# Moving the second layer's late modulation into the first context tile's attention, and alternating the order of the expert groups in layer 0

## The reference, cut to what matters

```python
for l in range(DEPTH):                      # DEPTH = 2
    sh_a, sc_a, gt_a, sh_f, sc_f, gt_f = split(silu(c) @ w_mod[l] + b_mod[l])     # w_mod[l]: 1024 x 6144
    ... the same for c_ctx, which modulates the context tokens
    hl = rmsnorm(xl) * (1 + sc_a) + sh_a;   xl = xl + gt_a * (mixers(hl, hc) @ w_out[l])
    hl = rmsnorm(xl) * (1 + sc_f) + sh_f;   xl = xl + gt_f * experts(hl)
    # context tokens likewise, in layer 0 only
def experts(h):                             # 16 experts, each takes its 64 best latent (32 best context) tokens
    gates, idx = top_k(softmax(h @ w_router))
    y = (silu(xs @ w_gate) * (xs @ w_up)) @ w_down * gates   # three 1024 x 1024 matrices for each expert
```

## Time and profile before

| | us |
|---|---|
| median of 3 runs (2144.3 to 2151.32) | 2147.86 |
| the profiled execution | 2151.53 |
| its span | 2149.7 |
| attention of layer 0, first scores to last | about 272 to 583 |
| gather and transposes before the experts of layer 0 | 632.7 to 645.4 |
| the 48 expert stages of layer 0 | 645.4 to 1187.5 |
| the 48 expert stages of layer 1 | 1674.9 to 2123.3 |

### The profile page before, as it was taken

The page is one execution under the profiler, slowest core; times in us unless marked ns, Lnnn a source line. Parts: engine busy times, 40 slices in busy tenths (PEclk is TensorE's granted clock), DMA queues, the critical chain, the costliest instruction groups (busy, mean ns, idle before and its releaser), DMA issues. The chain is left out here.

```text
span 2149.7 us, 27244 instructions
## 1 busy us (share of the span) xinstructions
PE 1969.2 (92%) x10872; PEld 931.5 (43%) x10872; DVE 664.1 (31%) x1746; ACT 529.6 (25%) x1222; POOL 156.6 (7%) x155
## 2 busy tenths in 40 slices
PE   5999989999979999999999899889997998888875
PEld 2436465556642332323323556455554333333322
DVE  3322345666540100101001632366665011110203
ACT  3211154665531000100100421165554110000001
POOL 1101010000010010020100101100001000000000
PEclk9999979999989999999999999999998999999998
DMA  9742020000089999999999402020017899999995
GB/s 353 291 159 81 0 79 1 1 2 1 36 332 414 423 364 418 378 390 421 364 414 421 150 20 79 17 82 1 21 40 286 352 427 426 426 427 427 427 427 217
DMA packets 90935, 515.66 MB, mean 240 GB/s; under 512 B 10594, under 2 KB 15628, under 8 KB 36540
## 3 DMA queue, kind: packets, MB, share of 16 engines
q1 hardware_dynamic: 84496, 493.29, 56.8%
q0 software_dynamic: 4416, 15.21, 2.4%
q10 hardware_dynamic: 1900, 5.43, 0.6%
HBM read 498.69 MB, written 15.20 MB: 239 GB/s over the span
## 5 line engine op out<-in xcount | busy, mean ns | idle before, releaser
L739 PE MATMUL psS<-arena 128*64 128x512 f32 (+9 forms) x4552 | 1158.5, 556 | 71.1 <-DMA arena<-in_w_up 22.0
L739 PEld LDWEIGHTS psS<-arena 128*64 128x64 f32 (+4 forms) x4552 | 456.1, 159 | 666.9 <-issue 585.9
L1961 DVE TENSOR_REDUCE mx<-psS 128x1 f32<-128x768 f32 (+2 forms) x200 | 165.5, 827 | 153.0 <-PE psS L739 151.3
L1307 ACT ACTIVATE arena<-psT 128x768 f32<-128x768 f32 (+7 forms) x261 | 150.1, 577 | 245.7 <-PE psT L742 232.0
L742 PE MATMUL psT<-ident,arena 128*128 128x128 f32 (+1 forms) x1036 | 172.7, 290 | 36.1 <-ACT arena L1307 9.1
L1307 ACT ACTIVATE arena<-psS 128x128 f32<-128x128 f32 (+5 forms) x158 | 61.8, 421 | 571.6 <-PE psS L739 525.7
L2145 DVE TENSOR_TENSOR arena<-arena,psS 128x512 f32<-128x512 f32 x32 | 20.6, 684 | 549.2 <-PE psS L739 549.2
L742 PEld LDWEIGHTS psT<-ident,arena 128*128 128x128 f32 (+1 forms) x1036 | 120.1, 145 | 135.5 <-issue 97.8
L739 PE MATMUL psT<-arena 128*32 128x512 f32 x1536 | 174.5, 595 | 0.0
L1307 ACT ACTIVATE arena<-psS,nb 128x768 f32<-128x768 f32 (+2 forms) x200 | 157.9, 792 | 1.4
L739 PE MATMUL psM<-arena 128*128 128x512 f32 x288 | 140.9, 611 | 0.0
(11 more groups left out here) (226 smaller groups left out, 1266.5 us busy)
## 6 DMA issues: line engine op xcount, KB each, us to landing
arena<-in_w_gate SPq DMA_DIRECT2D x117, 1024.0 KB, 21.3
arena<-in_w_up SPq DMA_DIRECT2D x116, 1024.0 KB, 22.5
arena<-in_w_down SPq DMA_DIRECT2D x116, 1024.0 KB, 25.9
arena<-in_w_mod SPq DMA_DIRECT2D x48, 1024.0 KB, 7.2
arena<-in_w_in SPq DMA_DIRECT2D x6, 2048.0 KB, 7.8
arena<-in_w_out SPq DMA_DIRECT2D x8, 512.0 KB, 7.8
arena<-in_w_out SPq DMA_DIRECT2D x2, 2048.0 KB, 15.4
normed_rows<-arena ACTq DMA_DIRECT2D x8, 512.0 KB, 7.3
```

The source lines that it names most:

```text
L739: return nc.tensor.matmul(o, lhsT, rhs, start=start, stop=stop)
L1307: return nc.scalar.activation(o, i, f, **kw)
L1961: link(V.reduce_max(mx[:, par:par + 1], view(S, 0, P, 0, (512, 2), (1, n)), axis=AX.XY))
```

## The change

1. The 16 late chunks no longer pass through the expert ring. They are loaded into four slots in `w_out`'s place, from the end of the projections on, and multiplied at steps 0 to 11 of the first context tile's attention. ACT copies their rows at steps 6 and 12, PE and DVE turn them at steps 16 and 24. `w_out` is loaded after them, part by part, as the slots come free.
2. The router's bias moves from steps 3 and 5 to 7 and 8, layer 0's gates from 7, 9, 11, 13 to 9, 11, 13, 15.
3. In layer 0's expert stages the order of the groups alternates. A stage that begins with the context group waits for all four loads at once. The transposes of the hidden rows and of the next tokens are moved to match, the latter in pairs; ACT and DVE follow the new order 2, 0, 1 of the hidden tiles.
4. `AHEAD_OF_GATHER` goes; in layer 1 the last two slots of the ring wait for the second gather instead.

```diff
-GATE_AT = ((7, 9, 11, 13), (9, 11))
-BIAS_AT = ((3, 5), (7,))
+GATE_AT = ((9, 11, 13, 15), (9, 11))
+BIAS_AT = ((7, 8), (7,))
-LAST_MOD_AT = {"turn": 13, "columns": 14}
+LATE_AT = {0: (0, 1), 1: (2, 3), 2: (4,), 3: (5,), 4: (6,), 5: (7,), 7: (8, 9), 8: (10, 11), 9: (12,), 10: (13,), 11: (14, 15)}
+LATE_ROW_AT = {6: 0, 12: 1}
+LATE_TURN_AT = {TURNS: 0, TURNS + 8: 1}
+LATE_BANK, LATE_TURN_BANK = (7, 5), 5
+LATE_SLOTS = 4
-TURN_AT = {(8, 1): (0,), (8, 2): (1,), (9, 0): (2,), (9, 1): (3,), (9, 2): (4,), (10, 0): (5,), (10, 1): (6,), (10, 2): (7,)}
+CLL, LLC = (2, 0, 1), (0, 1, 2)
+HIDDEN_AT = {(7, 0): 2, (7, 1): 0, (8, 2): 1}
+STAGE_ORDER = (LLC, CLL, LLC, CLL, LLC, CLL, LLC, CLL, CLL, LLC, CLL, LLC)
+TURN_AT = {(8, 1): (0, 1), (9, 1): (2, 3), (10, 2): (4, 5), (11, 1): (6, 7)}
...
+                def late_chunk(c):
+                    _, r, k = MOD_CHUNKS[MOD_FRONT * KD + c]
+                    if c >= LATE_SLOTS:
+                        sp.wait_ge(s_mused, MOD_FRONT * KD + c - LATE_SLOTS + 1)
+                    load(ar[:, late_slot(c):late_slot(c) + SLOT], A["w_mod"][L - 1, k * P:(k + 1) * P, r * 2048:(r + 1) * 2048], s_w[c % 8])
...
+                if l == 0:
+                    sp.wait_ge(z["proj"], NSTEP - TT)
+                    for c in range(2):
+                        late_chunk(c)
                 sp.wait_ge(z["proj"], NSTEP)
+                if l == 0:
+                    for c in range(2, 2 * KD):
+                        late_chunk(c)
+                for n, k in enumerate((4, 6, 0, 2)):
+                    if l == 0:
+                        sp.wait_ge(s_mused, (MOD_FRONT + 2) * KD - LATE_SLOTS + n + 1)
...
                     if l and j == NSLOT[l] - 2:
                         sp.wait_ge(z["fgev"], 4 * L)
+                        sp.wait_ge(s_g[1], 16 * L)
-                    if l == 0 and j == FIRST[l] + AHEAD_OF_GATHER:
-                        sp.wait_ge(s_g[2], 16)
...
+                    for c in LATE_AT.get(s, ()) if l == 0 else ():
+                        if c == KD:
+                            pe.wait_ge(z["me"], turns_through(PLANS[l], ("Q", 1, "B1")))
+                        late_mod(c)
+                    if l == 0 and s in LATE_TURN_AT:
+                        g = LATE_TURN_AT[s]
+                        pe.wait_ge(z["me"], turns_through(PLANS[l], ("Q", 2, "B1") if g else ("Q", 1, "C1")))
+                        mod_transpose(MOD_FRONT + g, LATE_TURN_BANK)
...
                     for x in turns:
+                        if l == 0 and x == ("Q", 1, "D"):
+                            pe.wait_ge(s_mrow, MOD_FRONT + 2)
+                        if l == 0 and x in (("T", 0, None), ("Q", 2, "D")):
+                            pe.wait_ge(s_mcol, MOD_FRONT + (1 if x[0] == "T" else 2))
                         turn(*x, values=v)
...
                         experts, n, col = range(QUAD), CAP_C, 256
-                        for e in experts if (q, st) == (NQ - 1, NSTAGE - 1) else ():
+                        for e in experts if order(l, q, st)[0] == g else ():
                             pe.wait_ge(*slot_filled(l, (q * NSTAGE + st) * QUAD + e))
...
+                    if l == 0 and s in LATE_ROW_AT:
+                        modulation_row(LATE_ROW_AT[s])
```

More of the change, by code:

```diff
@@ L596, in _ @@
                              A["w_router"][k].rearrange("(q p k) e -> p q (k e)", p=P, k=2), s_x)
+                if l == 0:
+                    sp.wait_ge(z["proj"], NSTEP - TT)
+                    for c in range(2):
+                        late_chunk(c)
                 sp.wait_ge(z["proj"], NSTEP)
[L599 to L606, removed]
+                if l == 0:
[4 more added lines that the diff above has]
+                        sp.wait_ge(s_mused, (MOD_FRONT + 2) * KD - LATE_SLOTS + n + 1)
+                    w = A["w_out"][l, k * P:(k + 2) * P, :]
+                    if k in (0, 6):
+                        for b in range(2):
+                            load(view(ar, 64 * b, 64, WOUT + k * D, (D, 2), (1, D)),
+                                 w[128 * b:128 * b + 128, :].rearrange("(a p) n -> p a n", p=64), z["wo"])
+                    else:
+                        load(ar[:, WOUT + k * D:WOUT + (k + 2) * D].rearrange("p (k n) -> p k n", k=2),
+                             w.rearrange("(k p) n -> p k n", p=P), z["wo"])
+                for j in range(NLOAD):
                     if j in OPEN[l]:
@@ L616, in _ @@
                         sp.wait_ge(z["fgev"], 4 * L)
+                        sp.wait_ge(s_g[1], 16 * L)
                     if l == 0 and j == NSLOT[l] - 1:
                         sp.wait_ge(s_xd, 16 * TT)
-                    if l == 0 and j == FIRST[l] + AHEAD_OF_GATHER:
-                        sp.wait_ge(s_g[2], 16)
                     last = j - NSLOT[l]
[L622 to L628, removed]
-                        load(ring(l, j), A["w_mod"][L - 1, k * P:(k + 1) * P, r * 2048:(r + 1) * 2048], s_w[j % NSLOT[l]])
-                        continue
-                    n = j - FIRST[l]
+                    if last >= 0:
+                        st, e = divmod(last, QUAD)
+                        sp.wait_ge(z["done"], groups_done(l, 0, st, e // 2) if l else stage_done(l, 0, st))
+                    n = j
                     if l == 0 and n == SUMS_STORED_AT * QUAD:
@@ L1164, in _ @@
                 gates(5, "fg", (0, 1, 2, 3))
-                late = range(MOD_FRONT * KD, (MOD_FRONT + 1) * KD) if l == 0 else ()
-                for n in late[:6]:
-                    late_mod(n)
                 pe.wait_ge(z["fgev"], 4 * l + 4)
                 for n in range(2):
-                    if n and l == 0:
-                        late_mod(late[6])
                     pe.wait_ge(z["dup"], 2 * l + n + 1)
                     tr(bank(4 + n, 0, P, 0, 48), ar[0:48, F["DUP"] + n * P:F["DUP"] + n * P + P], 48).then_inc(z["dupT"], 1)
-                for n in late[7:]:
-                    late_mod(n)
-                for g in (MOD_FRONT,) if l == 0 else ():
-                    mod_transpose(g, late_bank(g))
                 wc = l == 0
@@ L1210, in turn_hidden @@
                         last.then_inc(z["hp"], 1)
[L1211 to L1213 removed]
+                        free[6 + b] = (z["he"], 2 * hidden_turn(l, q, g) - 1 + b)
                 def combine(q):
@@ L1235, in combine @@
                         free[b] = (z["ce"], c * len(CJ) + n + 1)
-                    for m in last_late[4:] if l == 0 else ():
-                        late_mod(m)
                 def group(q, st, g):
@@ L1284, in _ @@
                     for st in range(NSTAGE):
-                        for g in last_order(l) if (q, st) == (NQ - 1, NSTAGE - 1) else range(NX):
-                            if st == 8 and g == 1 and wc:
-                                turn_hidden(q, 2)
+                        for g in (last_order(l) if not wc and (q, st) == (NQ - 1, NSTAGE - 1) else order(l, q, st)):
                             group(q, st, g)
-                            if st == 7 and g == 1:
+                            if wc and (st, g) in HIDDEN_AT:
+                                turn_hidden(q, HIDDEN_AT[st, g])
+                            if not wc and st == 7 and g == 1:
                                 turn_hidden(q, 0)
-                            if st == 7 and g == NX - 1:
                                 turn_hidden(q, 1)
@@ L1596, in _ @@
                 for q in range(NQ):
-                    for g in range(NX):
+                    for g in hidden_order(l):
                         act.wait_ge(z["done"], groups_done(l, q, 3, g))
@@ L2112, in _ @@
                         link(last)
-                for g in (MOD_FRONT,) if l == 0 else ():
-                    mod_columns(g, late_bank(g))
-                    dve.wait_ge(s_mcol, g + 1)
                 dve.sem_inc(z["lgev"], 1)
```

97 lines of the change are left out of this document (44 added, 53 removed).

## The result

The changed kernel takes 2164.41 us (median of 5 runs, 2161.1 to 2168.04), the kernel before 2147.86 beside it: ratio 1.007, 95% interval 1.0053 to 1.0086. That is 16.5 us slower. The forecast was 2152, with a range up to 2163, so the median lies 1.4 us beyond the range.

What follows compares the result with a forecast made beforehand. PE narrowly bounds layer 0's experts with DMA full, transfers bound layer 1's, a PE-DVE-ACT chain the first attention. 8.5 + 4.5 - 0.3 - 3.5 - 3.9 - 0.9 = +4.4 on 2151.5 gives 2155.9, as a median 2152; range 2139 to 2163.

Steps and rivals of the forecast that it cites:

- A: First tile's attention: taking in the late modulation costs +8.5 us, bounds +5 and +17.
- B: Layer 0's experts: alternation saves 7.7 us but adds waits for fourth loads; +4.5 us net, from -7.7 to +8.
- rival 2: First tile costs double, by clock at 0.50 or chunk waits: +17 there, step 12 above 317, 2161 us; chance 0.22.
- 16 - 3 - 3: First tile: 16 us of late work, less 3 for the router's bias moved, less 3 for the clock returning sooner.
- early recovery: First tile: denser work from step 0 brings the clock back before 292, 3 us off.
- the last lands at 306.0 at the earliest: First tile: with chunks 2 and 3 issued at 269.2, the last chunk lands at 306.0; 1.5 us charged for waits.
- Rival 1: Layer 0's experts: fourth loads arrive in time, alternation pays in full, -7.7 us, total 2140; chance 0.25.
- PE leads by only 0.7 us a stage: Layer 0's experts: a plain stage takes PE 10.6 us, its four loads 9.85 us.
- C: Seam at 1189, in `combine`: late chunks leave, PE idles 3.9 us and the clock may fall; -0.3 us, bounds -2.3 and +0.4.
- D: Token gathers before the experts: faster on a free queue, -3.5 us in layer 0 and -3.9 in layer 1.
- E: Layer 1: ACT's copy of 0.59 leaves a waiting chain, four transposes leave PE; -0.9 us.
- Rival 3: Gathers gain nothing, since their time is their own and not the queue's; sum +11.8 us, 2160; chance 0.08.

Runs made afterwards that it cites:

- late_only: The changed kernel with the alternation in layer 0's experts taken back; 2156.72 us, ratio 1.0043 to the kernel before.
- early_release: The changed kernel, with slots of experts 0 and 1 freed after the first latent group in context-first stages; 2167.36 us.
- late_narrow: late_only with all pieces multiplied, but over 64 columns instead of 512 in 12 of 16 late chunks; 2156.78 us.
- two_in_one: The changed kernel with narrow, 256 KB late chunks, context-first stages 1, 7, 8, 10 and silu in the order stage 3 ends; 2156.44 us.
- alt_only: The kernel before with the alternation alone; 2153.48 us, ratio 1.0028.
- guard_only: The kernel before, with layer 1's last two loads of the first ring filling waiting for both gathers; 2146.11 us, ratio 0.9991.
- late_light: late_only with only one of four pieces multiplied in 14 of 16 late chunks; 2156.82 us.
- late_small: late_only with late chunks of 256 KB instead of 1 MB, all matmuls kept; 2154.05 us.
- best1: guard_only with context-first stages 1, 9 and 11 of each quad and token turns in pairs; 2144.85 us, ratio 0.9986.
- before_half: The kernel before, with layer 0's expert loads bringing half their bytes from stage 4 of quad 0 on; 2141.97 us.
- alt_half: alt_only with layer 0's expert loads bringing half their bytes from stage 4 of quad 0 on; 2132.31 us.
- best2: guard_only with context-first stages 1, 7, 8, 10 and the changed kernel's places for hidden tiles and token turns; 2151.01 us, ratio 1.0010.

## Why the prediction came out as it did

**The sum.** The forecast was +4.4; it came to +16.5. The direction that I gave 0.34 happened. Two additions in the prediction are wrong: A's terms, 16 - 3 - 3 - 3 + 0.9 + 1.5, make 9.4 and not 8.5, and B's four quads, 1.1 + 1.1 + 0 + 2.1, make 4.3 and not 4.5. Put right, the forecast is 0.7 higher, which explains little of the miss. Term by term:

**A, late modulation in the first tile: +8.5 predicted, +13 measured** (325.4 against 312.3 to the end of attention; one by one +10.1, +13.3 and +16.0 in after, late_only and early_release). The mechanism stood: step 12 moved from 32 to 43 us after the first scores. At 316.15 it is 3 us past the announced 311 to 313 and just under rival 2's 317; in late_only and early_release it came at 316.9 and 319.2, 44.5 and 48.7 us after the first scores.

The small terms held. PE's waits for chunks were 1.9, 2.2 and 2.0 us for the 1.5 charged, its wait for the row copy 0.84 for 0.9. The other idle time up to step 12 fell from 3.7 to 1.5 us, where 3 were taken off. What was mis-sized is "16 - 3 - 3": PE's busy time up to step 12 is 28.4 us before and 39.0, 40.5 and 44.9 us in the three, so +10.5, +12.1 and +16.5 for that +10: near it in after, not in the others. The three execute the same matmuls there; what differs is the granted clock, 0.96, 0.92 and 0.82 in the mean of the stretch (0.68 before). Windows of PE from step 0's scores to step 12, before, then after, late_only and early_release:

```profile
271.68:303.94 32.26, 28.43 (x181) 0.68 0.45 126
```

```profile
273.46:316.15 42.69, 38.96 (x310) 0.96 0.94 369
```

```profile
272.39:316.93 44.54, 40.49 (x311) 0.92 0.91 355
```

```profile
270.56:319.22 48.66, 44.89 (x310) 0.82 0.87 327
```

The early recovery came, but the clock didn't stay: in 302 to 308 it was 1.00 in after, 0.74 in late_only and 0.72 in early_release. So a part of rival 2 is in the number. Why the clock falls in one execution and not in another stays open.

The stream was mis-sized too, in "the last lands at 306.0 at the earliest". In late_narrow chunk 15 was multiplied, on landing, at 311.78, although little PE work stood in its way. I had let the stream run from 269.2 on. But with four slots the fifth chunk can go out only when PE has multiplied the first, near 278, and the engines run short until then: 302 GB/s in 272 to 278 and 339 in 278 to 284 there, 115 in 278 to 282 in after, 425 and more only behind that. In after itself this bound isn't what PE waits for behind 290.

The experiments show two bounds that lie close together. With the stream shortened, 40.4 us are left to step 12; with PE's work shortened, 41.7; with both, 33.3. Each number is one execution, against 42.6 to 48.7 for the chunks in full size, and late_narrow has its 6 us at 1.2 GHz in it, so the first two are rough; 33.3 stands clear of the rest. It rules out that row copies, moved gates and moved turns make the 13 us. It doesn't show that they are free: two_in_one is 1 us above the kernel before, with the clock at 0.95 in the mean up to step 12 against 0.68, and with some late work left.

The other side of A held too: where the late work came from it had been free. From the end of attention to the first of the two top-k transposes all executions take 44.5 us, with or without the six chunks of 5.36 us; and from `combine` to layer 1 they take 17.3 to 18.4 against 17.9. So 16 chunks left places where PE waited for others, and came to one where it had no 13 us to spare.

**B, alternation: +4.5 predicted, +7.8 measured** (quads 550.1 in the mean of after, alt_only and early_release, 542.3 of before, guard_only and late_only; late_light, late_small and late_narrow, in the old order too, have 542.6 to 545.4). Its gain was as said, 7.7 against 8.4 with half loads. The Trainium skill, page "TensorEngine Tiling (Array Packing)", section Key Properties, says that a change of tiling mode drains the engine and gives no price. That a change costs something agrees with the traces: 8.4 us over 44 changes and the paired turns put it below 0.2 us each. The single waits held as well: 2.7 foretold at stage 7 of quad 0, 2.59; 2.7 at stage 5 of quads 1 and 2, 3.23 and 2.52; 2.8 at stage 7 of quad 3, 2.58. What was mis-sized is the sum of the costs. I took 12.2 us (4.5 and the 7.7 saved); the new waits alone are 13.9 in after, with 0.9 and 1.2 at stage 3 of quads 1 and 3, which I hadn't counted, and 1.7 more for the clock after the wait at 985.31. Rival 1, by which the loads would be there, is out.

There is a rule behind it that the prediction had only in part ("PE leads by only 0.7 us a stage"). From the first full point of quad 1 to that of quad 2 it is 136.0 us before (828.53 to 964.57), 137.0 in best1, 135.8 in two_in_one, 137.1 in alt_only (its waits at stage 5) and 137.5 in after. PE's savings, 3 to 8 us in the four quads and so 1 to 2 in this period, don't shorten it. early_release shows that issue isn't the limit at these points, and the window before 731.11 shows 429 GB/s. Over the whole period the DMA engines are busy for 0.98 before and 0.97 to 0.99 in the others, that is for 133 to 134 us in each. So in layer 0, too, the stream sets most of a quad's length, and PE chooses where it waits. The 1 to 4 us beside that stand for the most part in one place (share 0.80 in 890 to 910 before, 0.78 in after); what holds the stream there no run tests. Why the quads of two_in_one are 4 us longer than best1's is not settled; the waits at stage 7 of quads 0 and 3 (2.59 and 2.58), which best1 doesn't have, may be it, but no run tells them apart.

**C, the seam: -0.3 predicted.** From `combine` to layer 1's first transposes 17.28 us in after against 17.91, 17.3 to 18.4 in the others. PE idled 3.73 us at 1209.62, the clock fell to 0.53 in 1211 to 1214, as foretold (all had moved by 16 us), but for some 3 us and not 6.

**D, the gathers: -3.5 and -3.9 predicted.** Layer 0: from the top-k to the first expert matmul 12.0 to 12.4 us in after, late_only and early_release, 14.3 to 14.5 in before, guard_only and alt_only: -2.3. (Of the other four without the change, best1, before_half and alt_half have 13.8 to 14.0, best2 16.8.) The three gathers landed in 5.6 us after issue instead of 7.1, not in the announced 3.5 to 5, and PE waited 0.44 more for the second.

Layer 1, with E's copy and transposes in it: PE's wait was 4.8 to 5.3 us in every execution with the edit, near the announced 4 to 5, and 6.0 to 8.4 in the four without it. But from the first transposes of the layer to the first expert matmul it is 464.9 us in after, 466.7 in late_only and 466.8 in early_release, against 469.4 in before, 468.6 in alt_only, 468.3 in before_half and 465.4 in alt_half: -1.8 in the mean, for the -4.8 of D and E. The step that failed is that a shorter wait brings the experts' start forward by as much; executions differ by 2 us ahead of the wait, so -1.8 is rough. Rival 3 is out, and both terms were too hopeful, the second by more.

With these sizes, 13 + 7.8 - 0.3 - 2.3 - 1.8 = 16.4, near the 16.5 of the medians. With executions that differ by several us in A alone, that it meets so well is partly luck.

## What to carry to other kernels

Work that seems to cost PE time may stand in a place where PE waits anyway: take it out there and look at the stretch before pricing it somewhere else, for it is the new place that charges. Where a move brings PE work and a transfer into one stretch, work out both as bounds of that stretch; if they are about equal, shortening either gives little, and the test is to shorten both. Read such a stretch in several executions: here the same instructions took 42.7, 44.5 and 48.7 us by the clock that was granted. And where the stream of loads is full once in each period, measure the period from one full point to the next: while it stays the same, PE time saved between them turns into waiting.

## What the runs showed of the hardware

- Four matmuls with 32 columns of weights each, on four column ranges of the array, take the time of one: two records in 1.04 us, eight in 1.06; four in 1.90, sixteen in 1.92. The Trainium skill, page "TensorEngine Tiling (Array Packing)", section Key Properties, says that tiles work independently and in parallel; the trace agrees.
- A load that is issued earlier into a full stream doesn't land earlier: the same eight loads took 13.5 us from issue to landing in after and 16.3 in early_release, and PE's wait for the last of them ended 195.1 and 194.8 us after the first expert matmul.
- The granted clock fell behind waits for loads, but not behind each. After 2.91 us of waiting at 282.55 in late_narrow it was 0.50 in 284 to 290, after 2.00 at 285.49 in early_release 0.57 in 285 to 289; after and late_only, with waits of some 1.0 at most there, stood at 1.00. In the experts of after, a wait of 2.52 us at 985.31 was followed by such a fall, those of 2.59 at 731.11 and 3.23 at 847.83 were not.
- In layer 1 the stream of 1 MB loads ran at 426 GB/s for 438 us; in the first tile, with four slots, the loads began at 302 to 339 (272 to 284 in late_narrow) and then ran at 425.
